# A hybrid-attention encoder block with hierarchical MoE: query weights load last, one attention step is reordered, the last down chunk is split by columns

## The reference

```python
n = rms_norm(h, norm1_g)
p = n @ w_in            # (1024, 1536): qA 512 | kA 128 | vA 128 | qB 512 | kB 128 | vB 128
qa = rope(rms_norm(qa)) * scale;  ka = rope(rms_norm(ka));  oa = mixer_global(qa, ka, va)
ob = mixer_window(qb * scale, kb, vb, sink, rel_bias)   # |i-j| <= 128, bias from a table of 32 buckets
h = h + concat(rms_norm(oa), rms_norm(ob)) @ w_o
h = h + hier_moe(rms_norm(h))   # 32 experts: silu(x @ gate) * (x @ up), then @ down; 2 experts for a token
out = rms_norm(h, final_g)
```

## Time and profile before

| | |
|---|---|
| median of 3 runs | 575.41 us |
| the profiled execution | 575.66 us |
| its span, first to last instruction | 573.8 us |
| PE busy | 451.8 us (79%) |
| DVE, ACT, POOL busy | 117.3, 62.5, 28.2 us |
| moved by DMA | 218.72 MB, mean 381 GB/s |
| mean granted clock of TensorE | 0.901 of full |

### The profile page before, as it was taken

The page is one execution under the profiler, slowest core; times in us unless marked ns, Lnnn a source line. Parts: engine busy times, 40 slices in busy tenths (PEclk is TensorE's granted clock), DMA queues, the critical chain, the costliest instruction groups (busy, mean ns, idle before and its releaser), DMA issues.

```text
span 573.8 us, 6223 instructions
## 1 busy us (share of the span) xinstructions
PE 451.8 (79%) x2544; PEld 199.6 (35%) x2544; DVE 117.3 (20%) x282; ACT 62.5 (11%) x127; POOL 28.2 (5%) x58
## 2 busy tenths in 40 slices
PE   8999989999999994395999955765665765577565
PEld 3446767564535341041353511231113111322111
DVE  1017664252101212000212120012001200120204
ACT  1114233222010100000101000000000000000002
POOL 0052200040000000000000000000000000000001
PEclk9999999999999997887999987689868886897897
DMA  7989990855999999999999999999999999999982
GB/s 277 405 320 429 425 354 0 330 183 185 423 402 431 410 427 429 429 424 433 424 430 423 431 426 429 426 428 427 429 426 426 433 423 434 422 429 426 420 342 75
DMA packets 25342, 218.72 MB, mean 381 GB/s; under 512 B 5304, under 2 KB 6584, under 8 KB 13280
## 3 DMA queue, kind: packets, MB, share of 16 engines
q1 hardware_dynamic: 21072, 215.36, 89.9%
q10 hardware_dynamic: 4240, 2.94, 1.7%
HBM read 217.23 MB, written 1.06 MB: 380 GB/s over the span
## 4 chain that ended last, share of the span: by engine, by line
PE 54%; DMA 40%; SPq 2%; DVE 2%; issue 1%; POOL 0%; ACT 0%; POOLq 0%; DVEq 0%; ACTq 0%
PE bank L1266 20%; DMA ring<-in_w_gate_dram 14%; DMA ring<-in_w_down_dram 14%; DMA ring<-in_w_up_dram 12%; PE bank L1281 8%; PE bank L1056 7%; PE bank L1125 4%; PE bank L1317 3%; PE bank L1237 3%; PE bank L1115 2%; SPq L400 2%; PE bank L1104 1%; PE bank L1093 1%; PE bank L1037 1%; PE bank L1048 1%
## 5 line engine op out<-in xcount | busy, mean ns | idle before, releaser
L1266 PE MATMUL bank<-ring,region_x 128*32 128x512 f32 (+1 forms) x1024 | 162.3, 683 | 79.8 <-DMA ring<-in_w_up_dram 47.0
L1266 PEld LDWEIGHTS bank<-ring,region_x 128*32 128x32 f32 (+1 forms) x1024 | 47.3, 130 | 186.7 <-issue 186.7
L1281 PE MATMUL bank<-ring,region_q 128*32 128x512 f32 (+1 forms) x512 | 81.7, 684 | 29.7 <-DMA ring<-in_w_down_dram 28.1
L928 DVE TENSOR_TENSOR h<-h,bank 128x512 f32<-128x512 f32 x40 | 27.5, 688 | 116.5 <-PE bank L1317 116.5
L1281 PEld LDWEIGHTS bank<-ring,region_q 128*32 128x32 f32 (+1 forms) x512 | 23.4, 129 | 79.9 <-issue 73.2
L1056 PE MATMUL bank<-ring,region_x 128*128 128x512 f32 x96 | 42.2, 594 | 0.0
L1237 PE MATMUL bank<-region_q,region_t 128*128 128x128 f32 x320 | 39.8, 278 | 0.3 <-DVE region_q L901 0.3
L1237 PEld LDWEIGHTS bank<-region_q,region_t 128*128 128x128 f32 x320 | 37.3, 192 | 7.8 <-issue 7.8
L1317 PE MATMUL bank<-region_x,region_q 128*128 128x512 f32 x80 | 38.9, 619 | 0.0
L922 DVE TENSOR_TENSOR region_q<-region_q,bank 128x512 f32<-128x512 f32 x10 | 6.9, 688 | 119.4 <-PE bank L1266 119.4
L1125 PE MATMUL bank<-ring,region_q 128*128 128x512 f32 x64 | 28.9, 597 | 0.0
(11 more groups left out here) (183 smaller groups left out, 246.4 us busy)
## 6 DMA issues: line engine op xcount, KB each, us to landing
ring<-in_w_up_dram SPq DMA_DIRECT2D x31, 2048.0 KB, 33.8
ring<-in_w_gate_dram SPq DMA_DIRECT2D x28, 2048.0 KB, 32.5
ring<-in_w_down_dram SPq DMA_DIRECT2D x27, 2048.0 KB, 34.9
ring<-in_w_in_dram SPq DMA_DIRECT2D x8, 768.0 KB, 12.5
ring<-in_w_down_dram SPq DMA_DIRECT2D x12, 512.0 KB, 18.0
ring<-in_w_o_dram SPq DMA_DIRECT2D x2, 2048.0 KB, 11.9
ring<-in_w_gate_dram SPq DMA_DIRECT2D x8, 512.0 KB, 7.2
ring<-in_w_gate_dram SPq DMA_DIRECT2D x4, 1024.0 KB, 9.8
```

The lines of the kernel that those rows point to most:

```text
L928: dve.tensor_tensor(part, part, ps[SC0 + k % 2][:], ALU.add).then_inc(sc_free, 1)
L1266: last = pe.matmul(ps[bank][rows, :], xgT[:, c, rows], slots[fill_slot(f + a)][:, c * F:(c + 1) * F], start=(c == 0), stop=(c == KC - 1))
L1281: last = pe.matmul(ps[GD0 + half][rows, :], hT[:, c, rows], slots[fill_slot(f + a)][:, c * D + 512 * half:c * D + 512 * half + 512], start ...
```

## The change

1. **Start.** The gain columns `gT` are issued on ACT's queue rather than first on SP's. SP loads columns 512 to 1535 of each `w_in` chunk (512 KB instead of 768), then `x`, the constants and the rope table, and last the 512 query columns of all chunks in one DMA of 2 MB, `w_qa_in`, for which PE waits before `global_q(0, ...)`. PE multiplies zeros three times in place of four, and the product of the bias line stands behind the products of chunk 1. Five small loads on ACT's queue (gains, sink, router bias) come after the line's store.
2. **Attention.** `maxima(4)` moves from the head of step 4 on DVE to step 3, ahead of `mix_out` and `rotate(1)`. On PE the transposes of tile 1's A queries move ahead of `weigh_v(3)`.
3. **End.** The last piece is split into two column halves of chunk 3 (`LAST_PIECES`, now four pieces, 16 DMAs instead of 12). PE makes the products of half 0, multiplies by a constant once on either side of them, makes the scatter of (tile 0, half 0), then the products of half 1 and the three other scatters. The scatters use four PSUM banks. ACT copies both halves out. The squares go in the order of `LAST_ORDER`, into `silu_sb`; the gain of the first half tiles is multiplied by POOL and DVE ahead of time; the last step of the mean is DVE's, both inverse roots are POOL's, ACT scales two half tiles and DVE the two others, and three stores (SP two, ACT one) replace four.

```diff
-LAST_PIECES = ((0, 1), (2,), (3,))
+LAST_PIECES = (((0, 1), 0, D), ((2,), 0, D), ((3,), 0, D // 2), ((3,), D // 2, D))
+LAST_ORDER = ((0, 0), (1, 0), (0, 1), (1, 1))
@@ sync
-            sp.dma_start(gT[:], gain_cols).then_inc(gain_in, 16)
             for c in range(KC):
                 if c < 4:
                     sp.dma_start(xT[:, 2 * c:2 * c + 2, :], x_cols[:, 2 * c:2 * c + 2, :]).then_inc(xT_in[c], 16)
-                sp.dma_start(w_in_sb[:, c, :], w_in_c[c]).then_inc(w_in_in[c], 16)
-                if c == 5:
-                    for t, arrived in enumerate((x_in, x1_in)):
-                        sp.dma_start(h[:, t, :], x_t[t]).then_inc(arrived, 16)
+                sp.dma_start(w_in_sb[:, c, 512:IN_W], w_in_c[c][:, 512:IN_W]).then_inc(w_in_in[c], 16)
+            for t, arrived in enumerate((x_in, x1_in)):
+                sp.dma_start(h[:, t, :], x_t[t]).then_inc(arrived, 16)
             sp.dma_start(cst[:], consts).then_inc(consts_in, 16)
             sp.dma_start(rope_in, rope).then_inc(rope_in_sem, 16)
+            sp.dma_start(w_in_sb[:, :, 0:512], w_in_qa).then_inc(w_qa_in, 16)
             sp.wait_ge(bias_in, 16)
...
-            for k, (t, cols) in enumerate(HALVES):
-                sp.wait_ge(out_ready, k + 1)
-                sp.dma_start(out_t[t][:, cols], final_out[:, t, cols]).then_inc(stored, 16)
+            sp.wait_ge(act_out, 1)
+            sp.wait_ge(out_ready, 1)
+            sp.dma_start(out_t[0], final_out[:, 0, :]).then_inc(stored, 16)
+            sp.wait_ge(out_ready, 2)
+            sp.dma_start(out_t[1][:, 512:1024], final_out[:, 1, 512:1024]).then_inc(stored, 16)
@@ gpsimd
+            pool.wait_ge(ssf_ready, 1)
+            pool.tensor_tensor(final_out[:, 0, 0:512], h[:, 0, 0:512], final_gb[:, 0:512], ALU.mult).then_inc(gained_t0, 1)
...
+            pool.tensor_tensor(rstdf[:, 0:1], rstdf[:, 0:1], neg_half[:, 0:1], ALU.pow).then_inc(rstdf_ready, 1)
+            pool.wait_ge(mean_ready, 1)
+            pool.tensor_tensor(rstdf[:, 1:2], rstdf[:, 1:2], neg_half[:, 0:1], ALU.pow).then_inc(rstdf_ready, 1)
@@ scalar
+            down_out(UNITS - 1)
...
+            for t, gained in enumerate((gained_t0, gained_t1)):
+                act.wait_ge(gained, 1)
+                act.wait_ge(rstdf_ready, t + 1)
+                act.activation(final_out[:, t, 0:512], final_out[:, t, 0:512], ACT.Copy, scale=rstdf[:, t:t + 1]).then_inc(act_out, 1)
@@ vector
             for s in range(8):
-                if s != 3:
+                if s not in (3, 4):
                     maxima(s)
...
                 if s == 3:
+                    maxima(4)
                     mix_out(1, 0, 1)
                     rotate(1)
@@ tensor
-            multiply_zeros(2)
-            pe.wait_ge(onehot_in, 32)
-            pe.matmul(ps[7][0:8, :], relb_sb, onehot_sb, start=True, stop=True).then_inc(line_ready, 1)
-            multiply_zeros(2)
+            multiply_zeros(3)
...
                 last = qkv(0, QB, c, 2)
+                if c == 1:
+                    pe.wait_ge(onehot_in, 32)
+                    pe.matmul(ps[7][0:8, :], relb_sb, onehot_sb, start=True, stop=True).then_inc(line_ready, 1)
...
+            pe.wait_ge(w_qa_in, 16)
             global_q(0, range(0, 4))
...
+            last_products(0)
+            last_products(1)
+            multiply_constants(1, TR)
+            last_products(2)
+            multiply_constants(1, TR)
+            last_scatter(0)
+            last_products(3)
+            last_scatter(1)
+            last_scatter(2)
+            last_scatter(3)
```

102 lines of the change are left out of this document (61 added, 41 removed).

## The result

The changed kernel takes **571.83 us** (median of 20 runs, 569.38 to 574.48) against 575.68 of before (20 runs, 573.39 to 577.88): ratio **0.9935** (95% interval 0.9921 to 0.995), 3.7 us faster. Forecast were 568.5 and a range up to 571.5. The direction was right, the gain a little over half of the 6.9 us, and the median lies 0.3 us outside the range.

What follows compares the result with a forecast made beforehand. PE and its waits were taken to bound the kernel to about 134 us, DMA to 559.3, then a 14.5 us tail. Start 1.4 + attention 1.8 + tail 3.9 - 0.2 = 6.9 us gave 568.5, range 566.0 to 571.5.

Steps and rivals of the forecast that it cites:

- Start, 1.4: Start: QKV begins at 7.3 instead of 10.3 us; 3.0 less 0.9 bias line less 0.7 clock gains 1.4 us.
- The 0.7 set aside for the clock: Start: PE's clock may still rise only at 10.3 us, losing 1.5; half of that, 0.7 us, was deducted.
- The rival that the start gives nothing: Start: chunk lands at 8.5 us and the clock stays low; total gain 5.5 or 5.0, 570.4 us; chance 0.08.
- Attention, 1.8: Attention: PE's waits of 1.06 us before step 4's transposes and 0.78 before step 6's scores go; 1.8 us gained.
- The stream moves with PE: Expert loads: a microsecond won before 134 us moves them one earlier; rival that they don't loses 3.2, 571.7, chance 0.05.
- the query columns: Before global_q: rival that the late 2 MB query load makes PE wait 18 us, 11 slower, 586; chance 0.04.
- the second rival: Last loads: each small transfer costs its own time, last landing 5.6 us later, total gain 1.3, 574.1; chance 0.05.
- the 0.2 taken off: Last 2 MB of loads: four more DMAs and 2 KB rows slow the stream, costing 0.2 us (0 to 0.5).
- The tail, 3.9: After the last landing: split piece, reordered squares, shared scaling and fewer stores end at 569.9 instead of 573.8; 3.9 us gained.
- The tail's gain from the clock, 0.5: Last down products: without the 3.05 us pause they run at the faster clock, about 0.5 of the tail's 3.9 us.
- the median is 0.25 lower: Whole kernel: the median lies 0.25 us below the profiled execution, so 568.8 becomes a forecast of 568.5.
- The rival of a tail at 1.2 GHz (571.5): Tail: products, constants and first scatter at the low clock cost 3 us more; tail gain 0.9, total 3.9; chance 0.08.

Runs made afterwards that it cites:

- e8: The kernel before, unaltered, run again for a second trace: 576.41 us, ratio 1.0016 (10 runs).
- e17: The kernel before, unaltered, another trace: 32.81 us from the start of the last up products to the end; no total time given.
- e2: The kernel before with only the attention part (maxima of step 4 and query transposes moved up): 573.89 us, ratio 0.9963.
- e6: The changed kernel without the 512 KB store of token tile 0: 570.56 us, ratio 0.9897.
- e1: The kernel before with only the start part (w_in loads, ACT's first loads, zeros, bias line): 573.64 us, ratio 0.9961.
- e14: The changed kernel with three instead of four constant products before the rank products, one more trace: 573.71 us.
- e11: The changed kernel without its two constant products at the end: 571.12 us, ratio 0.9914.
- e12: The changed kernel, unaltered, run as the level for its set: 571.76 us, ratio 0.9924.
- e15: The changed kernel, unaltered, another trace: 570.31 us.
- e16: The changed kernel, unaltered, another trace: 571.41 us.
- e13: The changed kernel with three instead of four constant products before the rank products, another trace: 570.86 us.
- e4: The changed kernel, unaltered, run again for a second trace: 571.55 us, ratio 0.9915.
- e18: The kernel before, unaltered, another trace: 94.14 us from the first transpose after QKV to unit 0's first product; no total time given.
- e10: The changed kernel with three instead of four constant products before the rank products: 572.42 us, ratio 0.9923 (9 runs).

## Why the prediction was off

Unaltered traces averaged, four of before (spans 573.8, 572.8, 572.5, 573.7) and five of after (567.6, 570.4, 568.3, 568.5, 569.6), in us:

| Stage | before | after | gain | forecast |
|---|---|---|---|---|
| start to the first transpose after QKV | 37.5 | 35.8 | 1.7 | 1.4 |
| to unit 0, attention's waits | | | 1.86 | 1.8 |
| to unit 0, falls of the clock | 0.04 | 0.68 | -0.6 | none |
| unit 0 to U | 407.7 | 407.9 | -0.2 | none |
| U to the end | 34.0 | 32.4 | 1.6 | 3.9 - 0.2 |
| span | 573.2 | 568.9 | 4.3 | 6.9 |

- *Start, 1.4.* Right, with the mechanism, and somewhat too low (1.98 in the pair of profiled executions): QKV's first row at 7.08 (forecast 7.3). The 0.7 set aside for the clock was too much: PE was at the high clock from its first QKV row (12 rows in 5.39 us), and what varies is before, whose first transpose came between 37.0 and 37.8: in e8 and e17 four passes of zeros behind the bias line took 1.98 us, where the first trace has 3.36, and QKV began at 8.6 and 9.0. The rival that the start gives nothing fell.
- *Attention, 1.8.* Right: 1.87 in the trace, 1.6 in e2's median, no new wait.
- *The stream moves with PE.* Right: the last landing was nearly 4 us earlier in the trace, and U exactly 4.0. That rival, the query columns (landed at 30.5, wanted after 35.8) and the price of small transfers fell too. The Trainium skill's rule of 1 MiB or more per DMA (DMA: Bandwidth & Descriptors, Rules for kernel authors) shows as 0.2 to 0.3 us here, the shift of the last landing when pieces of 512 KB, already below it, were halved; the 5.6 us of the second rival were not there. So the 0.2 taken off was right as a size, but it fell where nothing waited for it: half 1 was later still by PE's own chain.
- *The tail, 3.9: this step failed.* The forecast, from U: half 1's products at 559.6 - 539.35 = 20.25, the last scaling ended at 28.05, the end at 30.55. The trace: 20.74, 28.36 and 32.25. (a) "the store and the end keep their 573.8 - 571.3 = 2.5" was the large error: 3.9, **1.4 us**. Before, each of four stores was issued behind its own scaling, over 2.9 us; now 1 MB goes out within 0.6 us. I had cut the scaling from 1.41 to 0.7 and left out what that does to the queue behind it. e6 shows half of it; the other half stays open. (b) "PE goes on without a pause" was true, but its chain of piece, constants, half 0, constants and scatter is longer than I made it. From start to start, the constants took 0.95 and 0.86 (forecast 0.7 and 0.75), half 0 0.99 (0.9) and the scatter 1.05 (0.95): **0.5 us** with the piece's own shift of 0.05, and this chain sets half 1. (c) From half 1 to the scaling's end it was 7.6 us, forecast 7.8; right.
- *The tail's gain from the clock, 0.5, was too small, and it counted before's slow products as a fixed cost.* Against e17 and e1 they cost 1.5 to 1.6 us, which is most of the 2.2 us that the end gained between the two profiled executions; the new order of squares, scalings and stores gave little. And e17 shows that before sometimes escapes them (U to the end 32.8), so that the mean gain of the end is 1.6, less than the 2.2 of the two profiled executions.
- *The forecast of the median from one profiled execution.* I took "the median is 0.25 lower" over from before, as if a change left the spread alone. The changed kernel's executions reach lower and spread as wide; the profiled one, at 569.48, missed the sum of 568.8 by only 0.7, since start and attention gave 0.7 more than forecast and the stages in between 0.1 or 0.2, but the median lies 2.35 above it. So of the 3.3 us between the forecast of 568.5 and the median, 0.7 are the sum's and 2.6 this step's; over the means of the traces, where it plays no part, the tail is the large error, 1.6 for 3.7. The five unaltered traces show 1.3 of this in the mean: 0.7 falls of the clock between QKV and unit 0, which before did not show and no rival had named, 0.4 between unit 0 and U, 0.15 at the end. The rest lies in executions without a trace. The rival of a tail at 1.2 GHz (571.5) named the nearest thing; what traces show is a half clock in part of the last up products, behind their wait of nearly 6 us (up products 8.4 to 9.9 us), in e14 and e11 in the down products too, and never in the scatters of the changed tail.

What stays open: why the clock falls there with the changed start (and once with the attention alone) and not in the kernel before; the start may matter only by the earlier time at which PE comes there, or by the gain's DMA, which lands late in six of its nine traces and in one of before's five. A longer pause is neither needed (e2, e12, e15 and e16 fall while PE is busy) nor enough (e13). Where the gain lands late and the clock holds until the rank products, the pause is 1.0 to 1.2 us instead of 0.84 (e1, e4, e6, e11, e18), but e18 had no fall. The Trainium skill (TensorE: Matmul & The Clock Gate, What's actually happening) says that the gate's watch is free-running and not tied to a kernel's start; executions of one kernel that differ as e10 and e13 do agree with it, but that page alone doesn't tell the two starts apart. Nor did I find what moves unit 0 to U by up to 1.6 us (407.4 to 409.0, both kernels alike).

## What to carry to other kernels

When the last compute of a kernel is made shorter or split over engines, price the stores again as well: they then leave together, and the bytes that had left behind the arithmetic wait behind each other. When a change makes a transfer land early enough, follow the consumer's own instruction chain in durations from the trace, since it becomes the bound, and then every fall of the clock that the wait used to hide is paid. Before a clock gain is priced, compare executions of the same kernel with and without it: here most of what the new end won against one trace was a slow stretch that another execution of the old kernel did not have. Forecast a median from several traces where a kernel's executions spread by more than the change, and ask of each stretch without slack what a half clock there costs.

## What was not expected of the hardware

- TensorE's granted clock fell to 0.50 (1.2 GHz) in the gather after pauses of only 1.0 to 1.8 us among small products (128x32, 128x1), and in four executions (e2, e12, e15, e16) with PE at 2.00 of 2 us busy, where windows of 2 us show 0.50 to 0.65. One kernel with one pause (e10, e13) took 6.71 and 3.81 us for the same 32 rows.
- Splitting the last 2 MB into eight transfers of 256 KB moved the last bytes by only 0.2 to 0.3 us, from U + 19.3 to 19.4 to U + 19.5 to 19.7. (Unsplit, PE got the last piece at U + 19.93 to 19.99 in six traces, but at 20.76 in e1.) The DMA rate falls over the last 4 us in either case (182 and 117 GB/s in the last two stretches of 1 us after, 205 and 66 before).
- Three stores, 1 MB in all, issued from two queues within 0.6 us, took 2.7, 3.2 and 3.5 us; two of 256 KB 2.5 and 2.6; one at a time 2.0.
